# A two-block fp32 network on one core: how the first stage is started and fed, and the order at the second mixer's entry

## The chip, the cores and the metric

The kernel runs on one core of a Trainium2 chip, in one launch. The metric is the device time of that launch in microseconds (us), lower being better, as the median of several runs. The core has five engines, each of which runs its own instructions in order: TensorE (PE, matmuls; its weight loads are shown apart as PEld), VectorE (DVE), ScalarE (ACT), GpSimd (POOL) and SyncE (SP, which here only issues DMA transfers). They wait for one another and for transfers through semaphores.

## The reference

256 tokens of width 1024 go through two blocks, after each other. The part that matters here is the first block, two layers deep:

```
mem_n = rmsnorm(mem, mem_norm)                       # 256 memory rows of 1024
for i in range(2):
    mem_kv = mem_n @ w_mem_kv[i];  mk, mv = split(mem_kv)
    h = rmsnorm(x, norm_mix[i])
    if i == 0:                                       # first mixer: short convolution
        u, b_gate, c_gate, q_mem = split(h @ a_w_in[i])
        v = c_gate * u
        y_tok = b_gate * (w[0]*v[s-2] + w[1]*v[s-1] + w[2]*v[s])
    else:                                            # second mixer: windowed attention
        q, q_mem = split(h @ b_w_q[0])
        y_tok = swa_sinks(q, k_band, v_band, ...)    # k, v from rmsnorm(x, kv_norm) @ w_kv
    y_mem = mem_attention(q_mem, mk, mv)             # softmax(q_mem mk / 8) mv, 4 heads
    x = x + concat(y_tok, y_mem) @ w_out
    x = x + (silu(h2 @ w_gate) * (h2 @ w_up)) @ w_down
```

where `rmsnorm(x, g) = x / sqrt(mean(x*x) + eps) * g`. The second block (an mLSTM mixer, then a sparse attention mixer) is not touched.

## The kernel before

**The stream of weights.** All large weights come as 272 units of 128 x 1024 fp32 (512 KB) in the order of their use. A unit `u` is loaded by SP into one of three buffers `raw`. ACT then copies it to `wh` in a shorter fp32 format (`split`, line 1121), and DVE writes the rest, `wl = raw - wh` (`low`, line 1573). `wh` and `wl` have six buffers each. A product is three matmuls: `wh` with the high part of the activations, `wh` with their low part, `wl` with the high part (lines 497 to 499). A projection unit is 8 slices of the contraction, so 24 matmuls of 256 columns.

ACT and DVE prepare unit u+4 when they come to unit u (`ahead_of`). SP asks for unit u when `wl` of unit u-3 is done, since both use the same `raw` buffer. All that SP issues goes through one queue of transfers, in order; ACT issues the four pieces of `xT` on a second queue.

**The first stage.** The activations come transposed (`x0T`, 1 MB in four pieces); ACT makes their high part `hxa` (line 1143), DVE their low part (line 1584). The scale 1/rms is applied behind the projection, so the matmuls need only the columns of gains (`cols`). The scale of `x` is made by ACT from a second copy of x by tokens (`square`, line 1153; square root, line 1168), inverted by DVE (line 1601) into a diagonal (line 1607) that PE spreads to all partitions (`rrow`, line 580). DVE copies it to `R` (line 1613). The projections of the stage are listed in order in `A_PRE`:

```
A_FIRST = [("qm", 0), ("qm", 1)] + _trip(0)
A_PRE = A_FIRST + _trip(1) + [("K", 0, 0), ("K", 0, 1), ("V", 0)]
```

with `_trip(j) = [("u", j), ("b", j), ("c", j)]`. Below they are called u0 to u11: u0 and u1 are `qm`, u2 to u4 and u5 to u7 the two triples, u8 and u9 the keys `K` of the memory, u10 and u11 the two halves of its values `V`. After a triple DVE runs the short convolution (lines 1808 to 1814), waits for ACT's copy `y` (line 1250) and writes its low part (line 1663). Behind u11 begins `attend`, with the scores of the memory heads (line 645).

The memory comes transposed (`mem`), and is split into `hxm` as x is, two slices behind each of u1 to u4. Its norm is made from the transposed copy too: ACT squares it (`xsq`, line 1331), GpSimd adds the squares up (`sum_squares`, line 2269), PE sums over partitions (`sumsq`, line 561, behind u8), ACT takes the root (line 1148), DVE inverts a tile of 128 x 256 into `Rm` (line 1618), and PE turns it into a column for V (`turn_r`, line 587, behind u11; `take_rcol`, line 1648).

**The second mixer's entry.** `B_PRE` is K0, K1, V0, q0, q1, and `attend` then takes one more query projection per pair of heads, q2 to q7, all into PSUM bank 7. So PE can begin q3 only when DVE has taken q2 out of that bank. For a pair DVE makes the row maxima (`maxima`, lines 1705 to 1708), ACT the exponentials (line 1224), DVE the probabilities (`probs`, line 1722), PE turns them (`turn`, line 670).

The program has no scheduler: all orders are those in which the code is written.

Of the kernel before, what the change touches and what calls it, by code (L numbers as in the profile page):

```python
# [187 lines left out]
def build(nc, xT, x_d, memT, stream, cols_d, ident_d, causal_d, bias_d, swamask_d, rope_d, perm_d, sel_d, bd_d, mlw_d,  # L188
          gsel_d, gatew_d, w1_d, w2_d, rows_d, out):
    with ExitStack() as ctx:  # L190
# [299 lines left out]
        def _(pe):  # L490
# [66 lines left out]
            def sumsq(bank, n):  # L557

                pe.wait_ge(sq_summed, n + 1)
                for k in range(2):  # L560
                    mm = pe.matmul(ps[:, bank, 0:T], ones[:], xsq[:, k, :], start=(k == 0), stop=(k == 1))
                mm.then_inc(sumsq_ready, 1)

# [18 lines left out]

            def turn_r(r, norm, bank):

                pe.wait_ge(rms_ready, norm + 1)
                for st in range(2):
                    mm = pe.transpose(ps[:, bank, st:st + 1], r[0:1, st * P:st * P + P], ident[0:1, 0:1])
                mm.then_inc(rrow_turned, 1)
# [1946 lines left out]
```

## Time and profile before

| | |
|---|---|
| median of 3 runs | 974.5 us (973.46 to 975.05) |
| the profiled execution | 973.25 us, of which its span 971.5 us |
| PE busy | 938.9 us, 97% of the span |
| DVE / ACT / POOL busy | 666.8 / 532.7 / 76.5 us |
| first matmul | 8.41 us into the span |
| first scores of the memory (end of the first stage) | 49.15 us |

Times in the rows are from the span's start. "Idle before" is how long the engine had nothing to do before an instruction, with what ended that. "x3" after a row means three merged instructions, and the second number is then from the start of the first to the end of the last. Instructions of one engine overlap a little, so the step from one to the next is shorter than the time of one.

### The profile page before, as it was taken

Reading aid. Unit: us, or ns where it says so; the run is one execution under the profiler, and the core shown is the slowest. Engines: PE = TensorE matmul, PEld = TensorE weight load, DVE = VectorE, ACT = ScalarE, POOL = GpSimd, SP = SyncE. Lnnn points to the kernel's source line nnn. Section 1 sums busy time; section 2 is a strip of 40 time slices with the busy share of each in tenths; the row PEclk is TensorE's granted clock in tenths of the full one; section 3 lists DMA queues with packets and bytes.
Section 4 is the critical chain, followed back from the end, with each engine's and each line's share of the span. In section 5 each row is a group of like instructions: output and inputs, shape, how many; then the busy total and the mean of one; then the engine's idle time right before and its main releaser. Section 6 shows DMA issues by size and latency. Waiting matters only on the chain.

```text
span 971.5 us, 16072 instructions
## 1 busy us (share of the span) xinstructions
PE 938.9 (97%) x5864; PEld 815.0 (84%) x5864; DVE 666.8 (69%) x1120; ACT 532.7 (55%) x934; POOL 76.5 (8%) x100
## 2 busy tenths in 40 slices
PE   6999999999999999999999999999999999989987
PEld 6999888888888986888888889888988789988875
DVE  5978566465555896575454658975779867488883
ACT  7555465354545775654444548656454764267772
POOL 0100011111100000100000000000111008111100
PEclk9999999999999999999999999999999999999998
DMA  8555656666563523666565553432224565322221
GB/s 311 162 189 173 212 180 226 209 194 223 186 217 131 173 88 118 234 218 212 172 199 190 185 183 109 152 117 79 88 88 132 174 236 180 125 75 93 93 68 44
DMA packets 42811, 156.39 MB, mean 161 GB/s; under 512 B 4956, under 2 KB 5228, under 8 KB 42112
## 3 DMA queue, kind: packets, MB, share of 16 engines
q1 hardware_dynamic: 40320, 146.02, 45.7%
q0 software_dynamic: 1856, 8.51, 2.5%
q10 hardware_dynamic: 576, 1.05, 0.3%
q8 instruction: 40, 0.66, 0.3%
q14 instruction: 19, 0.16, 0.1%
HBM read 154.51 MB, written 1.05 MB: 160 GB/s over the span
## 4 chain that ended last, share of the span: by engine, by line
PE 81%; DVE 11%; ACT 4%; issue 2%; DMA 2%; POOL 0%; SPq 0%; DVEq 0%; ACTq 0%; POOLq 0%
PE ps L714 8%; PE ps L718 8%; PE ps L716 8%; PE ps L546 8%; PE ps L550 7%; PE ps L548 7%; PE ps L497 6%; PE ps L498 6%; PE ps L499 6%; DVE wl L1573 3%; PE ps L1064 2%; PE ps L1018 1%; PE ps L1039 1%; PE ps L729 1%; DVE cacc L1939 1%
## 5 line engine op out<-in xcount | busy, mean ns | idle before, releaser
L1573 DVE TENSOR_TENSOR wl<-raw,wh 128x1024 fp32r<-128x1024 f32 x272 | 333.8, 1244 | 121.4 <-ACT wh L1121 64.7
L1121 ACT ACTIVATE wh<-raw 128x1024 fp32r<-128x1024 f32 x176 | 183.6, 1056 | 99.4 <-DMA raw<-stream_dram 71.9
L497 PE MATMUL ps<-hxa,wh 128*128 128x256 f32 x672 | 197.3, 294 | 11.9 <-DVE hxa L1584 8.4
L498 PE MATMUL ps<-hxa,wh 128*128 128x256 f32 x672 | 191.0, 284 | 0.0
L499 PE MATMUL ps<-hxa,wl 128*128 128x256 f32 x672 | 191.0, 284 | 0.0
L497 PEld LDWEIGHTS ps<-hxa,wh 128*128 128x128 f32 x672 | 129.5, 193 | 23.0 <-issue 15.2
L714 PE MATMUL ps<-wh,hxa 128*128 128x512 f32 x352 | 139.1, 395 | 0.9 <-DVE hxa L1594 0.9
L718 PE MATMUL ps<-wl,hxa 128*128 128x512 f32 x352 | 137.3, 390 | 0.0
L716 PE MATMUL ps<-wh,hxa 128*128 128x512 f32 x352 | 137.0, 389 | 0.0
L546 PE MATMUL ps<-wh,y 128*128 128x512 f32 x336 | 132.3, 394 | 1.2 <-DVE y L1663 0.7
L550 PE MATMUL ps<-wl,y 128*128 128x512 f32 x336 | 130.9, 390 | 0.0
L548 PE MATMUL ps<-wh,y 128*128 128x512 f32 x336 | 130.8, 389 | 0.0
L498 PEld LDWEIGHTS ps<-hxa,wh 128*128 128x128 f32 x672 | 129.8, 193 | 0.1
L499 PEld LDWEIGHTS ps<-hxa,wl 128*128 128x128 f32 x672 | 129.7, 193 | 0.0
L1264 ACT ACTIVATE wh<-raw 128x1024 fp32r<-128x1024 f32 x96 | 100.0, 1058 | 53.5 <-DMA raw<-stream_dram 34.7
L714 PEld LDWEIGHTS ps<-wh,hxa 128*128 128x128 f32 x352 | 66.1, 188 | 14.3 <-issue 1.3
L718 PEld LDWEIGHTS ps<-wl,hxa 128*128 128x128 f32 x352 | 66.1, 188 | 14.1
L716 PEld LDWEIGHTS ps<-wh,hxa 128*128 128x128 f32 x352 | 66.2, 188 | 13.1
L546 PEld LDWEIGHTS ps<-wh,y 128*128 128x128 f32 x336 | 63.1, 188 | 16.1 <-DVE y L1663 1.7
L550 PEld LDWEIGHTS ps<-wl,y 128*128 128x128 f32 x336 | 63.1, 188 | 13.3
L548 PEld LDWEIGHTS ps<-wh,y 128*128 128x128 f32 x336 | 63.1, 188 | 12.8
L1757 DVE TENSOR_TENSOR y<-ps,y 128x512 fp32r<-128x512 f32 x22 | 15.2, 692 | 73.0 <-ACT y L1285 73.0
(349 smaller groups left out, 1271.4 us busy)
## 6 DMA issues: line engine op xcount, KB each, us to landing
raw<-stream_dram SPq DMA_DIRECT2D x272, 512.0 KB, 4.0
biasm<-bias_dram POOLq DMA_DIRECT2D x12, 192.0 KB, 4.4
w<-w_dram POOLq DMA_DIRECT2D x1, 2048.0 KB, 9.1
mlw<-mlw_dram POOLq DMA_DIRECT2D x1, 1056.0 KB, 5.9
x0T<-xT_dram ACTq DMA_DIRECT2D x4, 256.0 KB, 7.4
x<-x_dram SPq DMA_DIRECT2D x1, 1024.0 KB, 6.6
mem<-memT_dram SPq DMA_DIRECT2D x1, 1024.0 KB, 5.8
grow<-rows_dram POOLq DMA_DIRECT2D x2, 512.0 KB, 3.9
```

The source lines that it names most:

```text
L497: pe.matmul(o, wh[:, w_s, w_cols], act[hi], start=start, stop=False, skip_group_check=True)
L498: pe.matmul(o, wh[:, w_s, w_cols], act[lo], start=False, stop=False, skip_group_check=True)
L499: return pe.matmul(o, wl[:, w_s, w_cols], act[hi], start=False, stop=stop, skip_group_check=True)
L546: pe.matmul(o, y[:, yk, 0, tok], wh[:, s % RING, wc], start=first, stop=False, skip_group_check=True)
L548: pe.matmul(o, y[:, yk, 1, tok], wh[:, s % RING, wc], start=False, stop=False, skip_group_check=True)
L550: mm = pe.matmul(o, y[:, yk, 0, tok], wl[:, s % RING, wc], start=False, stop=last, skip_group_check=True)
L714: pe.matmul(o, hxa[:, k, 0, tok], wh[:, s % RING, wc], start=(k == 0), stop=False, skip_group_check=True)
L716: pe.matmul(o, hxa[:, k, 1, tok], wh[:, s % RING, wc], start=False, stop=False, skip_group_check=True)
L718: mm = pe.matmul(o, hxa[:, k, 0, tok], wl[:, s % RING, wc], start=False, stop=(k == KC - 1), skip_group_check=True)
L1121: act.activation(wh[:, v % RING, :], raw[:, v % RAW, :], ACT.Copy).then_inc(wh_ready, 1)
L1264: act.activation(wh[:, v % RING, :], raw[:, v % RAW, :], ACT.Copy).then_inc(wh_ready, 1)
L1573: dve.tensor_tensor(wl[:, s % RING, :], raw[:, s % RAW, :], wh[:, s % RING, :].bitcast(F32), ALU.subtract).then_inc(wl_ready, 1)
```

## The change

Five things are changed.

1. PE runs 20 matmuls of 128 x 128 on the constant `ones`, into bank 2, before it waits for u0.
2. SP waits for the second and third piece of x0T before it asks for weight units 1 and 2. Units 4 and 5 are both asked for ahead of `mem`, and behind `mem` comes a new transfer `memx`, the memory by tokens (1 MB more), ahead of unit 6.
3. The memory's norm is made by tokens from `memx`: ACT squares and sums it, takes the root of 128 x 2; DVE inverts that (`mrt`) and makes a diagonal; PE spreads it (`rrow(ROW_MEM, 2)`) where `sumsq` was, behind u8. The squares, GpSimd's three additions, `sumsq`, the inversion of 128 x 256 and `turn_r` are gone.
4. ACT loads the square root's table at the start, and in the first stage both ACT and DVE split a weight unit before they split slices of the memory.
5. At the second mixer's entry DVE takes q2 before it makes the low part of a weight unit, and ACT loads the exponential's table one weight unit earlier.

```diff
             for u in range(1, RAW):
+                sp.wait_ge(xT_landed[u], 16)
                 sp.dma_start(raw[:, u % RAW, :], stream[u]).then_inc(landed[u % RAW], 16)
...
             load(RAW + 1, RAW + 1)
+            load(RAW + 2, RAW + 2)
             sp.dma_start(mem[:], memT).then_inc(mem_landed, 16)
-            load(RAW + 2, RAW + 2)
+            sp.dma_start(memx[:], mem_d).then_inc(memx_landed, 16)
...
             pe.wait_ge(consts_set, 1)
+            for _ in range(WARM_UP):
+                pe.matmul(ps[:, 2, 0:P], ones[:], ones[:], start=True, stop=True)
...
                 if e == ("K", 0, 0):
-                    sumsq(2, 0)
-                if e[0] == "V":
-                    pe.wait_ge(ident_landed, 16)
-                    turn_r(Rm, 0, 4)
+                    rrow(ROW_MEM, 2)
...
+            act.wait_ge(consts_set, 2)
+            root_table()
             split(0)
...
                 if j == 4:
-                    for p in range(4):
-                        act.activation(xsq[:, 2 * p:2 * p + 2, :], mem[:, 2 * p:2 * p + 2, :], ACT.Square)\
-                            .then_inc(sq_ready, 1)
-                if e == ("K", 0, 0):
-                    root(0, 0, bank=2)
+                    act.wait_ge(memx_landed, 16)
+                    for t in range(2):
+                        act.activation(memx[:, t, :], memx[:, t, :], ACT.Square, accum_out=mssq[:, t:t + 1])\
+                            .then_inc(mssq_ready, 1)
+                    act.wait_ge(mssq_ready, 2)
+                    act.activation(mstd, mssq, ACT.Sqrt, bias=eps[:, 0:1], scale=1.0 / D).then_inc(mstd_ready, 1)
...
-            for e in B_PRE[2:]:
+            for e in B_PRE[2:-1]:
                 ahead_of(PB[e], e)
+            act.activation(warm, eps[:, 0:1], ACT.Exp)
+            ahead_of(PB[B_PRE[-1]], B_PRE[-1])
...
                     for e in fills[i] if i < len(fills) else []:
-                        ahead_of(plan[e], e)
-                        take_fill(e)
+                        if i == 0 and e[0] == "q":
+                            take_fill(e)
+                            ahead_of(plan[e], e)
+                        else:
+                            ahead_of(plan[e], e)
+                            take_fill(e)
...
+                if j == 6:
+                    dve.wait_ge(mstd_ready, 1)
+                    dve.reciprocal(mrt, mstd).then_inc(mrt_ready, 1)
+                    dve.wait_ge(mrt_ready, 1)
+                    diagonal(mrt)
                 if e == ("K", 0, 0):
-                    invert(0, Rm)
-                if e == ("V", 0):
-                    take_rcol(0, 4)
+                    rows(ROW_MEM, 2, Rm)
...
-            sum_squares(0)
```

SP's transfers at the start of the program, before (the row with x2 is units 1 and 2, the next ones are units 3, 4 and 5):

```order
L460 DMA raw<-stream_dram 128x1024
L461 DMA cols<-cols_dram 128x367
L463 DMA raw<-stream_dram 128x1024 x2
L468 DMA raw<-stream_dram 128x1024
L471 DMA ident<-ident_dram 128x128
L472 DMA x<-x_dram 128x2048
L468 DMA raw<-stream_dram 128x1024
L474 DMA mem<-memT_dram 128x2048
L468 DMA raw<-stream_dram 128x1024
```

and now, with what the transfers wait for:

```order
L461 DMA raw<-stream_dram 128x1024
L462 DMA cols<-cols_dram 128x367
L466 DMA raw<-stream_dram 128x1024 [waits xT_landed1]
L466 DMA raw<-stream_dram 128x1024 [waits xT_landed2]
L471 DMA raw<-stream_dram 128x1024 [waits wl_ready]
L474 DMA ident<-ident_dram 128x128
L475 DMA x<-x_dram 128x2048
L471 DMA raw<-stream_dram 128x1024 [waits wl_ready] x2
L478 DMA mem<-memT_dram 128x2048
L479 DMA memx<-mem_dram 128x2048
```

Units 1 and 2 now wait for pieces of x0T; unit 5 moved ahead of `mem`, and `memx` stands between `mem` and unit 6, which is the first transfer behind these rows in both.

DVE's instructions from the low part behind the first convolution to that of unit 11, before:

```order
L1663 TENSOR_TENSOR y<-t_y,y 128x256
L1573 TENSOR_TENSOR wl<-raw,wh 128x1024
L1626 TENSOR_TENSOR t_u<-ps,R 128x256
L1573 TENSOR_TENSOR wl<-raw,wh 128x1024
L1626 TENSOR_TENSOR t_b<-ps,R 128x256
L1573 TENSOR_TENSOR wl<-raw,wh 128x1024
```

and now:

```order
L1641 TENSOR_TENSOR y<-t_y,y 128x256
L1560 TENSOR_TENSOR wl<-raw,wh 128x1024
L1608 TENSOR_TENSOR t_u<-ps,R 128x256
L1560 TENSOR_TENSOR wl<-raw,wh 128x1024
L1815 RECIPROCAL mcol<-mcol 128x2
L1594 TENSOR_SCALAR diag<-ident,mcol 128x128 x2
L1608 TENSOR_TENSOR t_b<-ps,R 128x256
L1560 TENSOR_TENSOR wl<-raw,wh 128x1024
```

The memory's diagonal, for which PE waits behind u8, is made behind the low parts of units 9 and 10.

DVE's instructions at the second mixer's entry, from the first pair's scores with their bias on, before:

```order
L1705 TENSOR_TENSOR ps<-ps,biasm 128x2x384
L1706 TENSOR_REDUCE nmax<-ps 128x2
L1707 TENSOR_REDUCE nmax<-ps 128x2
L1708 TENSOR_TENSOR nmax<-nmax,nsinks 128x4
L1573 TENSOR_TENSOR wl<-raw,wh 128x1024
L1628 SCALAR_TENSOR_TENSOR qm<-ps,R 128x256
```

and now:

```order
L1687 TENSOR_TENSOR ps<-ps,biasm 128x2x384
L1688 TENSOR_REDUCE nmax<-ps 128x2
L1689 TENSOR_REDUCE nmax<-ps 128x2
L1690 TENSOR_TENSOR nmax<-nmax,nsinks 128x4
L1610 SCALAR_TENSOR_TENSOR qm<-ps,R 128x256
L1560 TENSOR_TENSOR wl<-raw,wh 128x1024
```

The last two changed places, and nothing else.

## Rows read from the trace of the kernel before

**Rows 1.** The page's busy times: engine, busy us (share of span), instructions.

```profile
PE 938.9 (97%) x5864; PEld 815.0 (84%) x5864; DVE 666.8 (69%) x1120; ACT 532.7 (55%) x934; POOL 76.5 (8%) x100
```

**Rows 2.** Waits of PE: total us, times, longest.

```profile
PE ps L887 <- ACT h_sq L1460: 1.5, 1, 1.5
...
PE ps L497 <- DVE qm L1628: 1.2, 1, 1.2
```

**Rows 3.** Timeline of PE, 8 to 15 us: start, duration, instruction, idle before.

```profile
8.41 0.55 PE L497 MATMUL ps<-hxa,wh 128*128 128x256 f32 x1 [8.41 <-DVE hxa L1584]
...
13.57 0.41 PE L498 MATMUL ps<-hxa,wh 128*128 128x256 f32 x1
13.78 0.41 PE L499 MATMUL ps<-hxa,wl 128*128 128x256 f32 x1
...
14.56 0.28 PE L498 MATMUL ps<-hxa,wh 128*128 128x256 f32 x1
14.68 0.28 PE L499 MATMUL ps<-hxa,wl 128*128 128x256 f32 x1
```

**Rows 4.** Timeline of ACT, 10 to 24 us (at 23.50: unit 6).

```profile
10.18 1.89 ACT L1143 ACTIVATE hxa<-x0T,cols 128x256 fp32r<-128x256 f32 x4 [1.66 <-DMA x0T<-xT_dram]
11.98 2.94 ACT L1121 ACTIVATE wh<-raw 128x1024 fp32r<-128x1024 f32 x3
15.40 1.06 ACT L1153 ACTIVATE ajunk<-x 128x1024 f32<-128x1024 f32 x1 [0.48 <-DMA x<-x_dram]
...
17.75 1.28 ACT L1168 ACT_TABLE_LOAD   x1
...
23.50 1.05 ACT L1121 ACTIVATE wh<-raw 128x1024 fp32r<-128x1024 f32 x1
```

**Rows 5.** Stretches: window, us, busy of the engines, granted PE clock, DMA share, GB/s.

```profile
0.00:5.70 5.70, 0.00 (x0) 0.00 (x0) 0.20 (x5) 1.61 (x2) 0.21 (x4) 1.00 0.63 190
...
8.00:14.00 6.00, 5.59 (x24) 5.27 (x24) 4.24 (x10) 4.26 (x9) 0.00 (x0) 1.00 1.04 416
```

**Rows 6.** Tile raw, 0 to 30 us: from issue to landing.

```profile
DMA to landing us min/median/max: 3.7/4.5/8.8
```

**Rows 7.** Timeline of DVE, 13 to 46 us.

```profile
13.05 3.50 DVE L1573 TENSOR_TENSOR wl<-raw,wh 128x1024 fp32r<-128x1024 f32 x3 [0.38 <-ACT wh L1121]
...
22.06 0.87 DVE L1584 SCALAR_TENSOR_TENSOR hxm<-mem,cols,hxm 128x256 fp32r<-128x256 f32 x2
...
32.00 1.07 DVE L1808 TENSOR_TENSOR cu<-t_u,t_c 128x256 f32<-128x256 f32 x1
...
37.76 1.22 DVE L1573 TENSOR_TENSOR wl<-raw,wh 128x1024 fp32r<-128x1024 f32 x1
...
42.28 0.42 DVE L1808 TENSOR_TENSOR cu<-t_u,t_c 128x256 f32<-128x256 f32 x1
...
45.42 1.22 DVE L1573 TENSOR_TENSOR wl<-raw,wh 128x1024 fp32r<-128x1024 f32 x1
```

**Rows 8.** Timeline of PE, 39 to 50 us.

```profile
39.12 0.36 PE L497 MATMUL ps<-hxm,wh 128*128 128x256 f32 x1 [0.18 <-DVE wl L1573]
...
48.45 0.25 PE L587 MATMUL ps<-ident,Rm 1*128 1x1 f32 x2 [0.46 <-DVE Rm L1618]
49.15 1.14 PE L645 MATMUL ps<-mk,qm 64*128 64x256 f32 x8 [0.45 <-DVE mk L1626]
```

**Rows 9.** Timeline of GpSimd, 30 to 36 us.

```profile
30.63 5.04 POOL L2269 TENSOR_TENSOR xsq<-xsq 128x512 f32<-128x512 f32 x3 [30.10 <-ACT xsq L1331]
```

**Rows 10.** Timelines at the second mixer's entry: ACT, DVE, PE.

```profile
330.93 1.06 ACT L1121 ACTIVATE wh<-raw 128x1024 fp32r<-128x1024 f32 x1 [2.19 <-DMA raw<-stream_dram]
...
335.63 1.22 DVE L1573 TENSOR_TENSOR wl<-raw,wh 128x1024 fp32r<-128x1024 f32 x1
...
337.24 0.39 PE L497 MATMUL ps<-hxa,wh 128*128 128x256 f32 x1 [1.23 <-DVE qm L1628]
...
340.69 0.88 PE L670 MATMUL ps<-ident,prob 128*128 128x128 f32 x6 [0.33 <-DVE prob L1722]
```

More of the change, by code:

```diff
@@ L38 @@
 RING = 6
+WARM_UP = 20
 RAW = 3
@@ L169 @@
 (Q_A, Q_FFN0, Q_KV, Q_FFN1, Q_FINAL1, Q_ML, Q_NSA, Q_FINAL2) = range(8)
-ROW_A, ROW_KV, ROW_ML, ROW_NSA = range(4)
+ROW_A, ROW_MEM, ROW_KV, ROW_ML, ROW_NSA = range(5)
 def swa_head(c, h):
@@ L224, in build @@
         Rm = own("Rm", [P, T])
-        std = own("std", [P, T])
+        region(T * 4)
         cols = own("cols", [P, NCOLS])
@@ L236, in build @@
         gain2 = own("gain2", [P, KC])
-        rcol = own("rcol", [P, 2])
+        mcol = own("mcol", [P, 8])
+        mssq, mstd, mrt = mcol[:, 0:2], mcol[:, 2:4], mcol[:, 4:6]
         ssq = own("ssq", [P, 8, 2])
@@ L266, in build @@
         gatew = place("gatew", E + 13824, [P, KC, 48])
+        memx = place("memx", C, [P, 2, D])
         qm = place("qm", Dr, [P, 8, T])
@@ L375, in build @@
             sem(n) for n in ("consts_set", "gain2_ready", "gw_ready", "bias_ready"))
-        x_ready, sq_ready, sq_added, sq_summed, sumsq_ready, std_ready, rms_ready, rrow_turned = (
-            sem(n) for n in ("x_ready", "sq_ready", "sq_added", "sq_summed", "sumsq_ready", "std_ready",
-                             "rms_ready", "rrow_turned"))
+        x_ready, memx_landed, mssq_ready, mstd_ready, mrt_ready = (
+            sem(n) for n in ("x_ready", "memx_landed", "mssq_ready", "mstd_ready", "mrt_ready"))
         x_turned, ssq_ready, std2_ready, rt2_ready, diag_ready, rrow_made, rrow_ready, x1_ready, out_ready = (
@@ L555, in accumulate @@
                 mm.then_inc(unit_done, 1)
[L557 to L562, printed above, removed]
             def turn_x(rnd, banks):
@@ L581, in rrow @@
                 mm.then_inc(rrow_made, 1)
[L583 to L588, printed above, removed]
             def attend(a, b, plan, fills, hx, out_plan, y0, slots):
@@ L1143, in high_pair @@
                     act.activation(hx[:, k, 0, :], src[:, k, :], ACT.Copy, scale=col(gain, k)).then_inc(hi_ready, 1)
-            def root(norm, e, bank=0):
-                act.wait_ge(sumsq_ready, norm + 1)
-                act.activation(std[:], ps[:, bank, 0:T], ACT.Sqrt, bias=eps[:, e:e + 1], scale=1.0 / D)\
-                    .then_inc(std_ready, 1)
             def square(q, t, junk=xjunk, src=x):
@@ L1321, in _ @@
             for j, e in enumerate(A_PRE):
+                ahead_of(PA[e], e)
                 if j == 1:
@@ L1817, in _ @@
             for j, e in enumerate(A_PRE):
-                if 1 <= j <= 4:
-                    lows(mem, hxm, "mem_norm", 1, 2 * j - 2, 2 * j)
-                if e == ("K", 0, 1):
-                    take_a(e)
-                ahead_of(PA[e], e)
                 if j == 0:
@@ L1826, in _ @@
                     diagonal(rt2[:, Q_A, :])
+                if e == ("K", 0, 1):
+                    take_a(e)
+                ahead_of(PA[e], e)
                 if j == 2:
@@ L1830, in _ @@
                         take_a(first)
+                if 1 <= j <= 4:
+                    lows(mem, hxm, "mem_norm", 1, 2 * j - 2, 2 * j)
+                if j == 6:
[3 more added lines that the diff above has]
+                    diagonal(mrt)
                 if e == ("K", 0, 0):
-                    invert(0, Rm)
-                if e == ("V", 0):
-                    take_rcol(0, 4)
+                    rows(ROW_MEM, 2, Rm)
                 if j >= 2 and e != ("K", 0, 1):
@@ L2261, in _ @@
         def _(pool):
-            def sum_squares(n):
-                for p in range(1, 4):
-                    pool.wait_ge(sq_ready, 4 * n + p + 1)
-                    q = xsq
-                    if p > 1:
-                        pool.wait_ge(sq_added, 2 * n + p - 1)
-                    e = nc.gpsimd.tensor_tensor(q[:, 0:2, :], q[:, 0:2, :], q[:, 2 * p:2 * p + 2, :], ALU.add)
-                    e.then_inc(sq_added if p < 3 else sq_summed, 1)
-            sum_squares(0)
             pool.wait_ge(unit_done, PF0["gu", 0, 0])
@@ L2513, in lay_out @@
         "memT": np.asarray(a["mem"])[0].reshape(T, KC, P).transpose(2, 1, 0),
+        "mem": np.asarray(a["mem"])[0].reshape(2, P, D).transpose(1, 0, 2),
         "stream": stream_units(a), "cols": cols, "ident": np.eye(P, dtype=f),
```

14 lines of the change are left out of this document (2 added, 12 removed).

## The prediction

> **What bounds the kernel now.** I began with the busy times of the page. PE works 97% of the span [rows 1], so a change gains only where PE stands still, where its clock is low, or where its work is taken away. The list of PE's waits has next to nothing under this change: the start, one wait of 1.2 us for a `qm` at the second mixer's entry, and nothing longer than 1.5 us anywhere once PE runs [rows 2]. Then I read the timeline of each engine at both places, beside the stretches with their transfer rate.
>
> *The start.* PE's first matmul comes at 8.41 us. Its steps are 0.21 us until 13.78, and 0.12 us at 14.56 and after [rows 3]: 256 columns in 0.21 us are 1.2 GHz, the lower of the two levels, although the granted clock column says 1.00 [rows 5]. That unit needs 24 x 0.12 = 2.9 us and takes from 8.41 to 14.0. It is also starved: the third piece of x0T arrives at 10.18, ACT comes to unit 1 only at 11.98 [rows 4], and DVE starts the low parts of units 1 to 3 at 13.05, 3.50 us for three, so 1.14 each [rows 7].
>
> *The rest of the first stage.* From 14.3 to 39 us PE waits nowhere, and then three times within 10 us: for a `wl` (39.12), for `Rm` (48.45), for `mk` (49.15), 0.2 to 0.5 us each [rows 8]. All three are DVE's. PE and DVE run neck and neck here, so a PE that comes earlier meets a DVE that doesn't. Behind 49.15 PE has no gap for 75 us, so the shift of that row is what the first stage is worth.
>
> **The change, step by step.**
>
> *Warm-up and loads.* No row shows such a product at the low clock. A projection's step of 256 columns is 0.21 us there; 128 columns of plain fp32 cost between half a step (0.11) and two (0.43, if fp32 goes in four passes), so 20 of them 2.1 to 8.5 us. I take the long end, since the program avoids plain fp32 for its large products. From 1.1 us on, 5.4 us at the low clock (as long as u0 had it) are 12.6 products, the other 7.4 take 1.6 us: done at 8.1, when u0's operands come. With the short end PE would stand cold from 3 us on and u0 would run as before, and even that costs nothing, because PE has 3.7 us to spare further down. For x0T: by 5.70 us 1.08 MB have moved (190 GB/s [rows 5]), that is unit 0 (0.52), `cols` (0.19) and 0.37 of x0T. The other 0.68 MB, now alone, take 2.1 us at the 0.33 MB/us of that stretch behind its first 2.4 us. So x0T is through at 7.8, its second piece lands at about 7.1 and its third at 7.9 (estimates, with 0.9 us from the last byte to the semaphore). Unit 1 is asked for at 7.1 and lands 3.7 us later, the least seen [rows 6]: 10.8. ACT 1.0, DVE 1.14 behind it: u1 starts on PE at 13.05 instead of 14.3. Gain so far 1.3 us.
>
> *What the queue carries next.* Since SP waits, the queue runs dry from 7.8 to about 8.5, and x lands 0.7 us later than at the 15.4 of [rows 4], at 16.0. From there to unit 6 the queue is full: units 4, 5 and 6 (1.57 MB), `mem` and `memx` (2.10 MB) are 3.67 MB, at 416 GB/s [rows 5] 8.8 us. **Unit 6 lands at 24.8** (24.1 without the dry spell). Before, ACT split it at 23.50 [rows 4]. The root's table load (1.28 us) has left ACT's path, but what it freed is spent waiting here.
>
> *DVE from there.* ACT splits unit 6 to 25.8, DVE's low part ends at 26.9. Behind it, in order: `R` 0.35; two `qm` 0.76; three pairs of memory slices at 0.79 (a pair is 0.87 with its overlap [rows 7]) 2.4; three takes 1.0; low parts of u7 and u8 2.3; the first convolution with ACT's copy; low parts of u9 and u10 2.3; a take 0.3; the inversion of two columns and the diagonal 0.65. The convolution with its copy took 5.76 us (32.00 to 37.76), the second one 3.14 (42.28 to 45.42) [rows 7]. The first lay beside GpSimd's three additions, 30.63 to 35.67 [rows 9]. Without them it is 3.1, so 2.6 us are gained. Sum 13.2, and 0.2 for gaps between dependent instructions: the memory's diagonal is ready at 40.3.
>
> *PE meanwhile.* From 13.05: three units 8.7, `rrow` 0.45, five units 14.4, so it stands behind u8 at 36.6 and waits there **3.7 us** for the diagonal, then 0.45 for `rrow`. u9 starts at 40.75, before at 39.12. This is what takes the 1.3 us back. Behind it u9, u10 and u11 take 8.75, as from 39.12 to 47.9 before. The old wait for `Rm`, `turn_r` and the wait for `mk` (47.9 to 49.15) are gone; `mk` is taken by 47.5. The scores start at 49.5 instead of 49.15: **+0.3 us**. `sumsq` (1.0 us of PE) was ahead of 39.12 and is contained in that comparison.
>
> *Cost on others.* ACT's two squares of `memx` (2.4 us) lie in idle time ahead of its copy for the convolution; the root keeps its table. Later low parts come earlier than before.
>
> *Second mixer.* q2 is taken at 335.63 + 0.4, so PE begins q3 at 336.1 instead of 337.24 [rows 10]: 1.1 us. But the next thing PE does is `turn` at 340.69, where it already waited 0.33 us for DVE's probabilities. DVE is busy without a gap from 335.63 through them, with the same instructions in another order, so they are ready at 340.64 as before. The 1.1 us move from one wait to the next. The exponential's table goes into ACT's 2.19 us of idle ahead of 330.93 [rows 10] and costs nothing; DVE does not wait for the exponentials there. **0 us.** Without the cover of that wait the swap would be worth 1.1.
>
> Sum: 973.25 + 0.3 = 973.6 for the profiled execution; the median of the runs is 1.25 above it, so 974.8.
>
> **Bounds.** Unit 6 is the price with most play, and DVE's chain hangs on it one to one: 24.1 without the dry spell gives -0.7 against 974.8, transfers 10% slower give +1.0. So this case spans 973.8 to 976.0. A measurement of this kernel tells 0.2% (1.95 us) from no change.
>
> **The rivals.**
>
> *A. Unit 6 isn't late* (faster). If it lands by 21.8, DVE goes from unit 5 and its slices straight on: low part of u6 done at 23.9, 3.0 us earlier, u9 at 37.8, scores at 46.5. Time 974.8 - 3.0 = 971.8. For it: the convolution's 2.6 us and the table's 1.28 us are real. Against: the bytes, which even at 416 GB/s from 8 us on can't be through by then. It can also come in part, or from a DVE chain shorter than I add up. 0.22.
>
> *B. The swap at the second mixer pays* 1.1 us: 973.7, which is no change measurable. For it: a wait does vanish. Against: [rows 10]. 0.05.
>
> *C. PE's wait behind u8 lowers its clock* (slower). It is 3.7 us by my sum; the longest that the trace has behind a running PE is 1.5 us [rows 2], and PE kept its fast step there, so nothing here shows where it would fall. If it falls, PE pays the start's price again: about 5.4 us at 0.21 instead of 0.12, so 25 matmuls x 0.09 = 2.3 us, and all on the path, since PE bounds from u9 on. Time 977.1. The point from which it decides is a wait somewhere above 1.5 us. The same side is reached if `memx` slows the queue by a fifth. The Trainium skill (TensorE: Matmul & The Clock Gate, Part 1) says that an idle PE goes back to 1.2 GHz; by that rule alone this rival would be the forecast, and the trace neither bears it out nor refutes it for a wait of this length. 0.16.
>
> *D. Forecast:* the start's gain is eaten behind u8. 0.57.
>
> **How the numbers follow.** The predicted time is D's, 974.8. D and B and the part of A that is half-way are within 0.2% (972.55 to 976.45): 0.60. A in full and its upper half: faster 0.22. C: slower 0.18, with the tail of D. The range goes from A's 971.8 to C's 977.1.
>
> **What would show it.** Right: u1 at about 13.0; ACT waiting for unit 6 until about 24.8; the first convolution at 3.1 us; PE idle by 3 to 4 us ahead of the `rrow` behind u8; scores near 49.5; at the second mixer a gap of about 1.5 us ahead of `turn` in place of the one ahead of q3. Wrong: unit 6 by 23; steps of 0.21 us behind u8; `turn` of the first pair well ahead of its old place.

## The result: 2.7 us slower

| | before | changed | ratio |
|---|---|---|---|
| median of 9 runs | 974.71 us (973.46 to 975.52) | 977.43 us (976.08 to 979.23) | 1.0033, 95% interval 1.0022 to 1.0043 |
| the profiled execution | 973.25 us, span 971.5 | 977.43 us, span 975.7 | |

The forecast was 974.8 us with a range to 977.1. The change is slower by more than the 0.2% that can be told from nothing, and it lies 0.3 us beyond the range. The profiled executions are 4.2 us apart, the medians 2.7: that of before was a quick one of its kind, and part of the story below is why. From the first scores to the end the two executions are alike (973.25 - 49.15 = 924.10 us and 977.43 - 53.22 = 924.21), so what sets them apart lies in the first stage.

### The profile page after: what moved, and what is told of

Its sections match the earlier page's. It is cut to its first block, busy times and chain, and to the rows that moved or that the text cites. A ratio compares the mean times of both kernels' runs of the same rounds, so it can differ in the third digit from the quotient of the medians.

```text
span 975.7 us, 16144 instructions
## 1 busy us (share of the span) xinstructions
PE 944.4 (97%) x5902; PEld 821.0 (84%) x5902; DVE 663.6 (68%) x1122; ACT 533.2 (55%) x935; POOL 71.2 (7%) x97
## 4 chain that ended last, share of the span: by engine, by line
PE 82%; DVE 10%; ACT 3%; DMA 3%; issue 2%; POOL 0%; DVEq 0%; SPq 0%; ACTq 0%; POOLq 0%
PE ps L704 8%; PE ps L708 8%; PE ps L706 8%; PE ps L550 7%; PE ps L554 7%; PE ps L552 7%; PE ps L501 6%; PE ps L502 6%; PE ps L503 6%; DVE wl L1560 3%; DMA raw<-stream_dram 2%; PE ps L1053 2%; PE ps L1007 1%; PE ps L1028 1%; PE ps L719 1%
## 5 line engine op out<-in xcount | busy, mean ns | idle before, releaser
L501 PE MATMUL ps<-hxa,wh 128*128 128x256 f32 x672 | 196.3, 292 | 5.7 <-DVE qm L1610 2.1
L503 PE MATMUL ps<-hxa,wl 128*128 128x256 f32 x672 | 189.9, 283 | 0.0
L501 PEld LDWEIGHTS ps<-hxa,wh 128*128 128x128 f32 x672 | 128.4, 191 | 16.9 <-issue 6.8
L503 PEld LDWEIGHTS ps<-hxa,wl 128*128 128x128 f32 x672 | 128.6, 191 | 0.0
```

What stands on the lines that cost most here:

```text
L501: pe.matmul(o, wh[:, w_s, w_cols], act[hi], start=start, stop=False, skip_group_check=True)
L503: return pe.matmul(o, wl[:, w_s, w_cols], act[hi], start=False, stop=stop, skip_group_check=True)
```

## The profile after

PE's timeline at the start, then around its place behind u8 (start, duration, instruction, idle before it). L501 to L503 are the three products of a unit, L577 is `rrow`, L635 the first scores.

```profile
8.54 0.36 PE L501 MATMUL ps<-hxa,wh 128*128 128x256 f32 x1 [0.43 <-DVE hxa L1571]
8.74 0.28 PE L502 MATMUL ps<-hxa,wh 128*128 128x256 f32 x1
8.86 0.28 PE L503 MATMUL ps<-hxa,wl 128*128 128x256 f32 x1
...
12.84 0.39 PE L501 MATMUL ps<-hxa,wh 128*128 128x256 f32 x1 [1.00 <-DVE wl L1560]
...
30.02 0.39 PE L501 MATMUL ps<-hxa,wh 128*128 128x256 f32 x1 [2.08 <-DVE qm L1610]
...
42.46 0.71 PE L577 MATMUL ps<-diag,ones 128*128 128x128 f32 x4 [3.54 <-DVE diag L1594]
...
43.52 0.42 PE L502 MATMUL ps<-hxm,wh 128*128 128x256 f32 x1
43.73 0.41 PE L503 MATMUL ps<-hxm,wl 128*128 128x256 f32 x1
...
46.50 0.41 PE L501 MATMUL ps<-hxm,wh 128*128 128x256 f32 x1
46.72 0.35 PE L502 MATMUL ps<-hxm,wh 128*128 128x256 f32 x1
...
53.22 1.13 PE L635 MATMUL ps<-mk,qm 64*128 64x256 f32 x8
```

The start does what it was forecast to do: the warm-up ends at 8.11 (forecast 8.1), u0 has steps of 0.12 to 0.14 us behind its first product (0.21 in [rows 3]), and u1 begins at 12.84 (forecast 13.05). But the scores stand at 53.22, where [rows 8] had 49.15 and the forecast 49.5. Between lie two idle stretches ahead of PE: one of 2.08 us that the forecast did not have, and one of 3.54 us at the forecast place (forecast 3.7), which ends 2.2 us later than forecast. Behind it the steps grow from 0.12 to 0.21 us for three microseconds.

The granted clock in stretches shows the same (window, length, busy PE, PEld, DVE, ACT, POOL with their instructions, granted clock, DMA share, GB/s):

```profile
40.00:42.00 2.00, 0.00 (x0) 0.00 (x0) 1.96 (x5) 0.65 (x1) 0.00 (x0) 1.00 0.17 51
...
43.00:44.00 1.00, 1.00 (x9) 1.00 (x8) 1.00 (x2) 0.04 (x1) 0.00 (x0) 0.72 0.59 127
44.00:46.00 2.00, 2.00 (x11) 2.00 (x11) 1.86 (x5) 1.02 (x1) 0.00 (x0) 0.50 0.96 270
46.00:47.00 1.00, 1.00 (x7) 1.00 (x6) 0.52 (x2) 0.41 (x2) 0.00 (x0) 0.58 0.59 193
```

0.50 is the lower of the two levels, 1.2 GHz. PE did nothing from 40 to 42, DVE was busy throughout: the wait is DVE's. DVE's own timeline says where its lateness comes from:

```profile
27.95 1.23 DVE L1560 TENSOR_TENSOR wl<-raw,wh 128x1024 fp32r<-128x1024 f32 x1 [3.49 <-ACT wh L1110]
...
35.98 0.43 DVE L1790 TENSOR_TENSOR cu<-t_u,t_c 128x256 f32<-128x256 f32 x1
...
39.12 1.22 DVE L1560 TENSOR_TENSOR wl<-raw,wh 128x1024 fp32r<-128x1024 f32 x1
...
41.92 0.48 DVE L1594 TENSOR_SCALAR diag<-ident,mcol 128x128 f32<-128x128 f32 x2
```

From the convolution (35.98 to 39.12 is 3.14 us, forecast 3.1) to the diagonal all is as summed up. What is late is the row at the top: it starts at 27.95, and the forecast had unit 6's low part end at 26.9. ACT above it, beside [rows 4]:

```profile
16.91 1.06 ACT L1136 ACTIVATE ajunk<-x 128x1024 f32<-128x1024 f32 x1 [1.62 <-DMA x<-x_dram]
...
26.86 1.06 ACT L1110 ACTIVATE wh<-raw 128x1024 fp32r<-128x1024 f32 x1 [2.92 <-DMA raw<-stream_dram]
```

x comes at 16.91 (forecast 16.0), unit 6 at 26.86 (forecast 24.8). SP's waits left the queue half empty from 8 to 9 us (246 GB/s, and 420 in the kernel before), so 3.83 MB had moved by 14.0 us where it was 4.31 before. From 14 us on it was full:

```profile
0.00:8.00 8.00, 6.87 (x40) 6.79 (x40) 1.42 (x7) 3.77 (x7) 0.20 (x4) 1.00 0.68 222
8.00:14.00 6.00, 4.57 (x35) 4.28 (x34) 5.46 (x12) 4.22 (x8) 0.00 (x0) 1.00 0.97 343
14.00:16.90 2.90, 2.90 (x26) 2.90 (x25) 1.46 (x2) 1.06 (x1) 0.00 (x0) 1.00 1.02 397
16.90:24.80 7.90, 7.90 (x69) 7.90 (x68) 3.90 (x7) 5.53 (x9) 0.00 (x0) 1.00 0.99 405
24.80:26.90 2.10, 2.10 (x20) 2.10 (x19) 0.00 (x0) 0.04 (x1) 0.00 (x0) 1.00 0.98 400
```

Added up, 4.99 MB have moved by 16.9. All transfers up to unit 6 are 8.12 MB (seven units 3.67, x0T, x, `mem` and `memx` 4.19, the constants 0.26); the other 3.13 MB at 405 GB/s are through at 24.6. So the count of bytes says 24.6, and the landing is at 26.9. By 26.9 some 9.03 MB had moved, 0.9 MB more than unit 6 needed, so units behind it were under way before its landing was reported. For x the same count (4.45 MB) says 15.6 and the landing is at 16.9, and for the second piece of x0T (1.24 MB with unit 0 and `cols` before it) it says 6.3, with SP's next request at 7.03: the lag grows from 0.7 to 1.4 and 2.3 us. The Trainium skill (DMA: Bandwidth & Descriptors, "Why a DMA increments its semaphore by 16 and not by 1") says that every engine reports its own share and that only all of them together mean landed. By that rule a landing is that of the slowest engine. The trace fits it: a fixed delay of the report could be no more than the 0.7 us of x0T's piece, so of the 2.3 us some 1.6 (an estimate, the difference of the two) would be engines that are behind. No view here shows the engines one by one.

At the second mixer's entry, PE beside [rows 10]; everything here stands 4.11 us later:

```profile
336.09 0.38 PE L501 MATMUL ps<-hxa,wh 128*128 128x256 f32 x1
...
344.80 0.88 PE L660 MATMUL ps<-ident,prob 128*128 128x128 f32 x6 [1.46 <-DVE prob L1704]
```

The 1.23 us ahead of q3 are gone, and the 0.33 us ahead of `turn` have become 1.46.

## The experiments

Batches 1 (e1 to e4), 2 (e5 to e8), 3 (e9 to e12) and 4 (e13 to e16) each shared a chip with runs of the kernel before, whose medians were 974.9, 974.17, 974.7 and 974.8 us.

| kernel | median, us | ratio to before (95%) | x | unit 6 | PE waits, us (at) | scores |
|---|---|---|---|---|---|---|
| before | 974.71 | | 15.40 | 23.50 | 0.18 (39.12) | 49.15 |
| changed | 977.43 | 1.0033 (1.0022 to 1.0043) | 16.91 | 26.86 | 3.54 (42.46) | 53.22 |
| e1 | 975.02 | 1.0003 (0.9994 to 1.0011) | 17.61 | 24.70 | 3.11 (40.28) | 49.56 |
| e2 | 973.95 | 0.9995 (0.9986 to 1.0003) | 17.01 | 26.55 | 1.57 (40.18) | 49.47 |
| e3 | 971.71 | 0.9966 (0.9953 to 0.9979) | 17.05 | 24.55 | 1.54 (38.18) | 47.47 |
| e4 | 976.07 | 1.0015 (1.0006 to 1.0024) | 16.84 | 26.58 | none behind u8 | 51.82 |
| e5 | 973.87 | 0.9997 (0.9988 to 1.0005) | 15.79 | 23.73 | 0.38 (39.50) | 49.52 |
| e6 | 978.17 | 1.0034 (1.0021 to 1.0046) | 17.37 | 26.41 | 3.52 (41.99) | 52.78 |
| e7 | 978.48 | 1.0040 (1.0027 to 1.0053) | 17.39 | 27.38 | 3.52 (42.96) | 54.72 |
| e8 | 974.52 | 1.0005 (0.9996 to 1.0014) | 17.67 | 23.87 | 1.96 (39.22) | 49.96 |
| e9 | 972.45 | 0.9979 (0.9967 to 0.9991) | 16.61 | 25.13 | 0.92 (39.18) | 48.46 |
| e10 | 973.54 | 0.9993 (0.9984 to 1.0003) | 15.26 | 23.93 | 0.41 (39.54) | 49.55 |
| e11 | 974.84 | 1.0004 (0.9994 to 1.0013) | 17.17 | 24.51 | 1.13 (41.06) | 51.07 |
| e12 | 977.69 | 1.0025 (1.0012 to 1.0037) | 16.87 | 26.48 | 3.52 (42.06) | 54.01 |
| e13 | 977.86 | 1.0034 (1.0021 to 1.0047) | 17.12 | 26.59 | 3.53 (42.19) | 53.87 |
| e14 | 971.94 | 0.9971 (0.9960 to 0.9983) | 16.60 | 23.64 | 0.77 (37.27) | 46.57 |
| e15 | 974.12 (one run) | | 16.28 | 24.09 | 0.97 (40.00) | 50.03 |
| e16 | 977.13 (one run) | | 17.59 | 25.19 | 1.13 (41.49) | 51.52 |

The last four columns are of the profiled execution: when ACT takes x and unit 6, PE's idle behind u8 with the start of what it waited for, and the first scores.

From the scores to the end the profiled executions hardly differ: 924.0 to 924.2 us in twelve of the eighteen, 924.8 in e2, e3 and e9, and 925.5 to 925.7 in e5, e6 and e16, the three in which PE's clock fell near 370 us (last section). So a shift of the scores is paid one to one, and what is left over is not of the first stage.

### What the late unit 6 costs, and the wait for the diagonal

My theory: `memx` ahead of unit 6 makes DVE late (+2), and PE stands for the diagonal behind u8 (+1.6 against a spread that comes one unit later), with the clock on top. The rival: the two are one cost, and mending either mends all.

**e1** moves `memx` behind units 6 and 7:

```diff
-            sp.dma_start(memx[:], mem_d).then_inc(memx_landed, 16)
-            with sp.Fori(1, UNITS // RING) as i:
+            load(RING, RING)
+            load(RING + 1, RING + 1)
+            sp.dma_start(memx[:], mem_d).then_inc(memx_landed, 16)
+            for u in range(RING + 2, 2 * RING):
+                load(u, u)
+            with sp.Fori(2, UNITS // RING) as i:
```

> The changed kernel, with memx asked for behind units 6 and 7 instead of ahead of unit 6. Theory (the extra megabyte delays unit 6, and DVE's chain to the memory's diagonal hangs on it one to one): unit 6 is split at about 24.3 us instead of 26.86, the diagonal is ready at 39.9 instead of 42.4, PE's wait behind u8 is about 3.1 us, and the scores come at 50.7 (49.2 if the clock stays up): total 974.9, or 973.4. Rival (DVE's chain is bound by its own work and the order of the transfers doesn't matter): 977.4 as before the edit.

**e2** moves the spread of the memory's scale on PE one unit back:

```diff
-                if e == ("K", 0, 0):
+                if e == ("K", 0, 1):
                     rrow(ROW_MEM, 2)
```

> The changed kernel, with PE's rrow(ROW_MEM) moved from behind u8 to behind u9; transfers unchanged. Theory (PE stands 3.5 us behind u8 only because it waits for the diagonal in order, and then pays 1.5 us at the low clock): the wait behind u8 shrinks to about 1.4 us (for the low part of u9), no step of 0.21 us behind it, scores at about 49.5 instead of 53.2, total 973.7. Rival (a late unit 6 delays everything behind it anyway): wait moves one place on, 976.5 or more.

**e3** does both:

> Both edits: memx behind units 6 and 7, rrow(ROW_MEM) behind u9. Theory: low part of u9 at 37.8, u9 starts right then, scores at about 47.0, total 971.2, which would beat both kernels. Rival (one of them alone takes all there is): 973.5.

**e4** leaves all in place and lets PE run 12 more of the constant's products while it waits:

```diff
                 if e == ("K", 0, 0):
+                    for _ in range(12):
+                        pe.matmul(ps[:, 2, 0:P], ones[:], ones[:], start=True, stop=True)
                     rrow(ROW_MEM, 2)
```

> The changed kernel, with 12 more products of the constant (128 x 128) on PE between u8 and rrow(ROW_MEM), into the same bank, so that PE works through its wait. Theory (part of the loss is the clock that falls behind the 3.5 us wait): no step of 0.21 us in u9, the diagonal no later, scores at 51.7 instead of 53.2, total 975.9. Rival (the low steps cost nothing since DVE bounds there): 977.4.

Measured, against the changed kernel's 977.43: e1 -2.4, e2 -3.5, e3 -5.7, e4 -1.4 us. The first two add up (5.9) within what the medians can tell, so they are two costs. In e1 the wait of 3.11 us was as expected and the clock stayed up behind it in the profiled execution; that one (973.58) is the fastest of the eleven, whose mean granted clocks go down to 0.995, so it need not have stayed up in all. In e4 PE works through the wait, and behind it has steps of 0.12:

```profile
39.98 2.84 PE L767 MATMUL ps<-ones 128*128 128x128 f32 x24
42.65 0.61 PE L577 MATMUL ps<-diag,ones 128*128 128x128 f32 x4
43.02 0.36 PE L501 MATMUL ps<-hxm,wh 128*128 128x256 f32 x1
43.22 0.28 PE L502 MATMUL ps<-hxm,wh 128*128 128x256 f32 x1
```

The diagonal is as late as ever, but the scores stand at 51.82 instead of 53.22: 1.4 us in the profile and 1.4 in the medians are the clock's price. That the clock falls because PE stands, and not because of anything else at that place, is thereby shown. (e4's clock did fall once, ahead of u6 at 29.74; that was over by 33.4 and cost nothing, as PE still came to the diagonal before DVE had it.) With unit 6 late but no fall behind u8, e4's median of 976.07 lies in the forecast's range, and so does e1's 975.02 with unit 6 two microseconds earlier; it took both to go beyond it. e3 beats the kernel before by 0.34% and the changed one by 0.6%.

### The second mixer, the warm-up, SP's waits

**e5** is the kernel before with part 5 of the change alone.

> The kernel before, with only the two edits at the second mixer's entry (q2 taken ahead of the low part, the exponential's table one weight unit earlier). Theory (the wait moves, DVE bounds): PE's wait of 1.23 us ahead of q3 is gone, a wait of about 1.5 us stands ahead of the first turn, which stays at 340.7; total as before. Rival (the vanished wait is a gain): total 1.1 us less than before.

973.87 against 974.17, a ratio of 0.9997 (0.9988 to 1.0005): nothing, as the term of 0 us had it. The row ahead of `turn` in e5 is `[1.47 <-DVE prob L1728]`, and 0.35 us of the wait ahead of q3 are left (336.72).

**e6** drops the warm-up (`WARM_UP = 0`).

> The changed kernel without the 20 warm-up products (WARM_UP = 0). Theory (PE has slack ahead of unit 6 and of the memory's diagonal): u0 runs at 0.21 us a step until about 13.9, u1 starts a microsecond later than 12.84, PE's two waits for DVE are shorter by as much, total 977.4 as with them. Rival (the warm-up gives its 2 us): 979.

978.17 us, with the wait of 3.52 us at 41.99 and scores at 52.78: the warm-up is worth nothing that can be measured. But u1 was not a microsecond later, as expected: PE's slow steps in u0 ended at about 11.1 us instead of 13.9, and u1 came at 12.85. So e6 does not test whether a later u1 would be absorbed; e7 does.

**e7** drops SP's waits for x0T (`sp.wait_ge(xT_landed[u], 16)`).

> The changed kernel without SP's waits for the pieces of x0T ahead of units 1 and 2. Theory (what counts is when unit 6 lands, and the waits leave the queue dry): u1 starts later, about 14.2, but x lands near 15.5 and unit 6 near 26 instead of 26.86; total 976.5. Rival (the start of u1 counts): 978.5 or more.

This one missed. u1 is late as expected (14.58), but x came at 17.39 instead of 15.5, unit 6 at 27.38 instead of 26, and the time was 978.48 instead of 976.5. That is the rival's number, but not for its reason: u1 is 1.7 us later, and PE's wait behind u8 is the same 3.52 us, so PE had that time to spare; the scores are late by the 0.5 us of unit 6 and by a longer stretch at the low clock (11.76 us from the spread to the scores, 10.76 in the changed kernel). And x is late without SP's waits too. Stretches of e7, and then the kernel before's:

```profile
0.00:8.00 8.00, 6.19 (x40) 6.00 (x40) 1.20 (x6) 3.54 (x6) 0.21 (x4) 1.00 0.72 223
8.00:14.00 6.00, 3.75 (x24) 3.16 (x24) 4.36 (x11) 4.28 (x8) 0.00 (x0) 1.00 1.04 410
14.00:15.00 1.00, 0.42 (x3) 0.42 (x4) 1.00 (x2) 1.00 (x2) 0.00 (x0) 1.00 0.34 139
15.00:16.00 1.00, 1.00 (x11) 1.00 (x10) 1.00 (x2) 0.16 (x1) 0.00 (x0) 1.00 0.55 98
```

```profile
0.00:8.00 8.00, 0.00 (x0) 0.00 (x0) 1.56 (x7) 3.63 (x5) 0.21 (x4) 1.00 0.74 227
8.00:14.00 6.00, 5.59 (x24) 5.27 (x24) 4.24 (x10) 4.26 (x9) 0.00 (x0) 1.00 1.04 416
14.00:15.00 1.00, 0.86 (x6) 0.67 (x6) 1.00 (x2) 0.92 (x1) 0.00 (x0) 1.00 0.32 131
```

What must have moved for x to be complete is 4.45 MB. By 14.0 us it was 4.24 MB in e7 and 4.31 before, so the queue had 0.2 and 0.14 MB to go, half a microsecond at full rate; x landed 3.4 and 1.4 us after 14.0. The tail flows at a third of the rate, with a DMA share of 0.34 and 0.32: it looks as if a few DMA engines were behind, and how far differs from one trace to the next. By 14.0 us e7 is 0.4 MB ahead of the changed kernel (3.83 MB), which is a microsecond at full rate, so the gap that SP's waits leave in the queue is real; in e7 the longer tail took more than that back.

**e8** is e3 with six additions of 128 x 256 on GpSimd, on a scratch tile, beside DVE's first convolution.

```diff
+            pool.wait_ge(lo_ready, 16)
+            for n in range(6):
+                pool.wait_ge(pool_chain, n + 1)
+                nc.gpsimd.tensor_tensor(pjunk[:], pjunk[:], pjunk[:], ALU.add).then_inc(pool_chain, 1)
```

> The kernel with memx late and rrow(ROW_MEM) behind u9 (971.7 us), with six additions of 128 x 256 by GpSimd beside DVE's first convolution, on a scratch tile that nothing reads. Theory (GpSimd's additions slow DVE's instructions beside them, as in the kernel before, where the convolution took 5.76 us and not 3.14): the convolution takes 5 us or more, the scores come 2 to 2.6 us later, total about 974. Rival (the slow convolution had another cause): 971.7.

DVE's timeline in e8, with GpSimd at work from 33.18 for 4.32 us:

```profile
33.47 0.61 DVE L1794 TENSOR_TENSOR cu<-t_u,t_c 128x256 f32<-128x256 f32 x1
34.11 0.59 DVE L1795 TENSOR_SCALAR t_y<-cu,cols 128x256 f32<-128x256 f32 x1
34.73 1.54 DVE L1797 SCALAR_TENSOR_TENSOR t_y<-cu,cols,t_y 128x256 f32<-128x256 f32 x2
36.31 0.72 DVE L1800 TENSOR_TENSOR t_y<-t_y,t_b 128x256 f32<-128x256 f32 x1
...
37.85 1.22 DVE L1564 TENSOR_TENSOR wl<-raw,wh 128x1024 fp32r<-128x1024 f32 x1
```

The convolution takes 4.38 us (33.47 to 37.85); in e3 the same stretch is 3.14 (33.67 to 36.81), its first four rows 0.43, 0.35, 1.01 and 0.42. So work on GpSimd does lengthen DVE's, here by 1.24 us. In the kernel before it is 2.6, which lie in the three rows that stand beside GpSimd's (1.07, 1.27 and 2.06 us for 0.42, 0.35 and 1.01 in its second convolution); the fourth, behind 35.67, is 0.43 again. The Trainium skill (GPSIMD Engine Reference, "Key points") has the two share their path to SBUF, with contention for DVE instructions that have two SBUF inputs or run in a certain mode; the row with a tile and a column as its inputs was lengthened as much (0.35 to 0.59), and no view shows whether it ran in that mode. The convolution missed the expected 5 us. That the scores (2.5 us behind e3's) and the median came out as expected is in part luck, since only 1.04 us of it is the later u9. The other 1.45 are the clock's: behind a wait of only 1.96 us, PE's steps went to 0.21 us:

```profile
39.22 0.36 PE L505 MATMUL ps<-hxm,wh 128*128 128x256 f32 x1 [1.96 <-DVE wl L1564]
...
40.25 0.38 PE L507 MATMUL ps<-hxm,wl 128*128 128x256 f32 x1
40.42 0.42 PE L505 MATMUL ps<-hxm,wh 128*128 128x256 f32 x1
```

### Why x, and with it unit 6, is late

**e9** is e3 without SP's waits.

> The kernel of e3 (transfer of the memory by tokens behind units 6 and 7, the spread behind u9), and SP no longer waits for pieces of x0T before it asks for units 1 and 2. By my theory the stretch from u1 to u9 is bound by the landing of unit 6 and by DVE behind it, and SP's waits only move u1: u1 1.7 us later (14.6), unit 6 within 0.5 us of e3's 24.55, scores within 0.5 us of e3's 47.47, and the time e3's 971.7. The rival is that the waits are worth what they seem in the comparison of the changed kernel with e7, about 1 us: scores at 48.5, time 972.8.

Scores at 48.46, 1.0 us behind e3, as the rival had it; the median of 972.45 lies 0.3 us from the rival's and 0.7 from mine, and the intervals of e3 and e9 overlap. A later u1 is not what costs here, since PE still waits 0.92 us for DVE at u9. Unit 6 came 0.6 us later than in e3 (25.13) and unit 7 1.1 later (27.46 for 26.32, behind a wait for its transfer). With one profile each, whether SP's waits make that difference or the variation told below is unclear.

**e10** is the kernel before with the square root's table loaded first.

```diff
+            act.wait_ge(consts_set, 2)
+            root_table()
             split(0)
```

> The kernel before, and ACT loads the square root's table ahead of its first weight unit instead of behind the squares of x. Nothing else. In all kernels with the changed start x landed at 16.9 to 17.7 us (SP's waits or not), in the two without it at 15.4 and 15.8. Theory T: the table's load at the start is what makes x late, since it is one of the few things that the changed kernel with no waits has and the kernel before has not. Then x lands at 17 or later here. Rival: it has nothing to do with it, and x lands at 15.4 to 15.8; the table's 1.28 us leave ACT's path and unit 6 is split up to 1.0 us earlier than at 23.50. The time by the rival is 974 to 974.5, since DVE is bound by other work; by T up to 1 us more.

**e12** is the changed kernel without that early load.

> The changed kernel, but ACT does not load the square root's table at the start; the load then stands in front of the root of x, as before the change. By theory T x lands at 16.0 (SP's waits alone) instead of 16.9, unit 6 is split by 25.9 and the scores are at about 52.3. By the rival x lands at 16.9 or later, the table's 1.28 us are taken out of the time in which ACT would wait for unit 6, and scores and time are as in the changed kernel: 53.2 and 977.4.

x at 15.26 in e10 and at 16.87 in e12, each where it was without the edit (15.40 and 16.91): the table's load has nothing to do with it, and being rid of it is worth nothing measurable in either (0.9993, 0.9984 to 1.0003; 977.69 against 977.43).

**e11** is the kernel before with one more input, which nothing reads:

```diff
         "memT": np.asarray(a["mem"])[0].reshape(T, KC, P).transpose(2, 1, 0),
+        "mem": np.asarray(a["mem"])[0].reshape(2, P, D).transpose(1, 0, 2),
         "stream": stream_units(a),
```

> The kernel before, with the memory by tokens as one more input in the chip's memory, ahead of the stream of weights, which no instruction reads. Only addresses of the inputs behind it move by 1 MB. Theory M: where the inputs lie decides how evenly the transfers go, and x lands at 17 or later here too. Rival: x lands at 15.4 to 15.8 and the time is that of the kernel before, 974.5. I hold the rival for likelier.

**e13** is the changed kernel, **e14** is e3, both with that input as the last one in place of ahead of the stream.

> The changed kernel, with the memory by tokens as the last of the inputs in the chip's memory instead of ahead of the stream of weights; the instructions are the same. Theory M (where the inputs lie makes x's landing late): x lands at 16.0 as forecast, unit 6 is split by 25.9, PE's wait behind u8 is about 2.6 us, and the time is 976.4 or, if the clock no longer falls, 975. Rival N (x's landing varies from execution to execution whatever the inputs): x at 15.5 to 17.7, time 977.4 as the changed kernel.

> The kernel of e3 (transfer of the memory by tokens behind units 6 and 7, the spread behind u9), with the memory by tokens as the last input. By theory M x lands at 16.0 and unit 6 up to 1 us ahead of 24.55; the scores come by 46.9 and the time is 971. By rival N time and scores as in e3: 971.7 and 47.5.

**e15** is the kernel before and **e16** is e11, each profiled once more.

> The kernel before, profiled once more. Its times spread from 973.3 to 976.7 in all the runs so far and the first profile was of an execution at the low end (973.25). By rival N a second execution may show x at 16.5 or later; one that takes 974.5 or more should show it, and one of 973.5 or less should show x by 15.8. By theory M x lands at 15.4 to 15.8 whatever the time, and what lengthens it lies elsewhere.

> The kernel of e11 (before, with an input that nothing reads ahead of the stream), profiled once more. Theory M: x lands at 17 again. Rival N: x anywhere from 15.4 to 17.5, at 15.8 or earlier where the time is 973.5 or less.

In e11 x came at 17.17, though its times are those of the kernel before. That looked like an effect of where inputs lie. e13 speaks against it: there all other inputs lie as in the kernel before, and x still came at 17.12. e14 is divided: its profiled execution has unit 6 0.9 us ahead of e3's and scores at 46.57, as theory M had it, but it is the fastest of its seven, and the median of 971.94 is e3's (971.71), as the rival had it. And e15 shows the kernel before with x at 16.28:

```profile
16.28 1.06 ACT L1153 ACTIVATE ajunk<-x 128x1024 f32<-128x1024 f32 x1 [1.30 <-DMA x<-x_dram]
```

Over six profiles with the old start (e10, before, e5, e15, and e11 and e16 with the idle input) x lands at 15.26, 15.40, 15.79, 16.28, 17.17 and 17.59. From 15.40 on, the later it is, the later are u9 (39.12 to 41.49) and the scores (49.15 to 51.52); e10 has the earliest x, but scores at 49.55. From 15.40 to 17.59 is 2.19 us, and the scores move by 2.37. So the landing varies by 0.9 us between two executions of one kernel (before and e15) and by 2.3 over kernels with the same transfers up to x, and is paid nearly one to one; e15, e11 and e16 took 974.12, 975.17 and 977.13 us where the first profile took 973.25 (1.5 of e16's are its fall of the clock near 370 us). The two with the idle input are the two latest, and with six profiles chance cannot be told from an effect of the addresses. With the new start x never came before 16.60 in any profile. That the start itself, rather than chance, holds it there was not shown: e7 and e9 have it without SP's waits, and had 17.39 and 16.61.

## Why the prediction was wrong, point by point

- **Warm-up and loads.** Right in size (done at 8.11 for 8.1, u1 at 12.84 for 13.05; 0.7 us from the last byte to the landing of x0T's second piece for the 0.9 assumed) and right that it is worth nothing: e6 and e7.
- **"Unit 6 lands at 24.8."** This is the step that failed: the term was mis-sized by 2.1 us, and its bounds of 24.1 and 25.8 did not hold it. The forecast went from a landing, x at 16.0, and added 8.8 us for 3.67 MB. Measured, x was 0.9 us later (16.91), and unit 6 came 9.95 us behind it, 1.1 more. Of these 1.1 the rate is 0.2 (405 GB/s for 416), and 0.9 is that unit 6 lagged its bytes by 2.3 us and x by only 1.4; the forecast took the lag to be the same. It was no single bad execution: in the seven profiles with these transfers up to unit 6 (changed, e2, e4, e6, e7, e12, e13) x comes at 16.84 to 17.39, and unit 6 9.0 to 10.0 us behind it. Why the lag grows stays open.
- **"x lands 0.7 us later, because the queue runs dry."** The queue does run dry: by bytes x is 1.1 us behind (0.48 MB at 14.0 us). But e7 without the waits landed x no earlier. How much of the 1.5 us between 15.40 and 16.91 is the gap and how much is variation was not shown.
- **DVE from there.** Right: 15.5 us from unit 6 on ACT to the end of the diagonal at 42.40 (forecast 24.8 to 40.3, 15.5), and the convolution 3.14 for 3.1. e8 shows that work on GpSimd lengthens it. All the lateness came in with unit 6, one to one.
- **PE's wait behind u8.** Right in place, late by 2.2, and its size (3.54 for 3.7) is luck. Not foreseen was the wait of 2.08 us at 30.02: u6 goes into the bank of u0 (bank 1), which DVE empties (`qm`) only behind the low part of unit 6. Without it PE would have stood behind u8 at about 36.8 and waited 5.6 us. With it DVE sets both ends, the start of u6 and the diagonal, so the wait is 3.52 to 3.54 us in all five profiles that have it, whenever u1 began. The wait at 30.02 cost nothing by itself, since it only takes from the one that follows.
- **Rival C, the clock.** I gave it 0.16 and it came, in every execution that I have of a wait of 3.52 to 3.54 us (changed, e6, e7, e12, e13); the mean granted clock of the changed kernel's nine runs is 0.995 to 0.996, before it is 0.997 to 0.999. From the spread to the scores e1 took 9.28 us at full clock (40.28 to 49.56), the changed kernel 10.76, e6 10.79, e13 11.68, e7 11.76 and e12 11.95. So the price is 1.5 to 2.7 us, around the 2.3 that I had worked out. The rival's 977.1 had unit 6 in time, and no case of the forecast had both costs; that is why the range ended below 977.43. The rule of the Trainium skill that I weighed there (TensorE: Matmul & The Clock Gate, Part 1) made this the forecast, and it was the better guide. I set it aside because the trace had no wait of that length; that was no reason to give it a small chance. And the bound of "somewhere above 1.5 us" does not hold for shorter waits that follow each other (0.85 and 0.90 us, last section).
- **Second mixer, 0 us.** Right: [rows 10] against the rows above, and e5.
- **Rival A, unit 6 in time.** It did not come: 26.86.
- **The base.** I added 1.25 us for the median and took everything else from an execution in which x was early. The changed kernel's profiled execution is its median (977.43), so that term, too, was off. The kernel before has executions with x later (e15: scores 0.9 us later), and its near kin e5 and e16 have some in which the clock falls near 370 us (1.5 us); how often each comes was not measured.

Together: 49.5 forecast, +2.1 for unit 6, +1.6 for the slower way from the diagonal to the scores (10.76 us for 9.2) is 53.2, as measured.

## What to carry to other kernels

Date a transfer in a full queue by its own landing, not by the byte count or by the landing of another: give what the trace shows between bytes and landing (here 0.7 to 3 us) as a range, and look at a second profile, if there is one, before resting a chain on a single landing. A wait that moves onto a running PE costs more than its length: where it is longer than any that the trace shows with the clock kept, sum it with the clock's price as well, together with the lateness that made it long, and let the two outcomes weigh alike. Here even waits of 1.9 us had that price at times. A scale that is applied behind the projection is needed only when the result is taken, so its spread can stand a unit later on PE; that alone was worth 3.5 us here, and with the extra megabyte asked for behind what DVE waits for, 5.7. A PSUM bank that is used again ties PE to the instruction that empties it: count its release among PE's waits.

## What the runs showed of the hardware

- The clock's fall does not go by the length of one wait. It fell behind 3.5 us (five profiles), behind 1.96 (e8) and behind 1.90 (e4, ahead of u6), and stayed up behind 3.11 (e1), 2.08 (the changed kernel, ahead of u6), 1.57 (e2) and 1.54 (e3). The rows of e4:

```profile
29.74 0.42 PE L501 MATMUL ps<-hxa,wh 128*128 128x256 f32 x1 [1.90 <-DVE qm L1612]
...
30.39 0.41 PE L501 MATMUL ps<-hxa,wh 128*128 128x256 f32 x1
30.60 0.41 PE L502 MATMUL ps<-hxa,wh 128*128 128x256 f32 x1
```

- At the second mixer, near 370 us, PE waits 0.85 and then 0.90 us in every one of the eighteen profiles; the clock fell in e5, e6 and e16 and stayed up in the other fifteen, the kernel before among them. The fall costs about 1.5 us (scores to end 925.5 to 925.7 for 924.1). The stretches of e16:

```profile
370.00:372.00 2.00, 1.10 (x8) 0.77 (x10) 1.97 (x7) 1.95 (x8) 0.00 (x0) 0.93 0.00 0
372.00:374.00 2.00, 2.00 (x12) 1.39 (x9) 1.12 (x6) 1.69 (x8) 0.00 (x0) 0.50 0.00 0
```

- Landings in one queue lie 0.7 (a piece of x0T) to 3 us (x in e7) behind the bytes, and differ by 0.9 us between two executions of one kernel (x, 15.40 and 16.28).
- GpSimd beside DVE lengthened its fp32 instructions by 1.4 to 1.7 times (0.43 to 0.61, 0.35 to 0.59, 0.42 to 0.72), those with one tile as input too. Beside the kernel before's additions of 128 x 512 it was 2.0 to 3.6 times (1.01 to 2.06, 0.42 to 1.07, 0.35 to 1.27).
